# Norm chains begun per residual tile, two norms from one set of tiles, 24 vector products moved into the heads, output in four pieces

## The reference

```python
def rmsnorm(x, g):
    xf = x.astype(jnp.float32)
    y = xf * lax.rsqrt(jnp.mean(xf * xf, axis=-1, keepdims=True) + EPS)
    return (y * g.astype(jnp.float32)).astype(x.dtype)
...
    mod = sc @ w_ada[l] + b_ada[l]
    sh1, sc1, ga1, sh2, sc2, ga2 = jnp.split(mod, N_ADA, axis=-1)
    h = _rmsnorm(x, g_mix[l]) * (1.0 + sc1[:, None, :]) + sh1[:, None, :]
    mix = _hybrid_mixer(...)                     # 8 heads: attention and an LRU; norms of both; w_out
    x = x + ga1[:, None, :] * mix
    h = _rmsnorm(x, g_ffn[l]) * (1.0 + sc2[:, None, :]) + sh2[:, None, :]
    x = x + ga2[:, None, :] * _peer(h, ...)      # top-k over product keys, 16384 experts
return _rmsnorm(x, g_final)
```

## Time and profile before

| | |
|---|---|
| median of 3 runs | 3832.76 us (3823.6 to 3842.07) |
| the profiled execution | 3838.9 us; span of its records 3837.2 |
| mean granted clock of TensorE | 0.962 |
| busy: PE, DVE, ACT, POOL | 3595.6, 2425.1, 1333.5, 390.2 us |
| HBM read, written | 791.66 MB, 24.18 MB |

### The profile page before, as it was taken

The page is one execution under the profiler, slowest core; times in us unless marked ns, Lnnn a source line. Parts: engine busy times, 40 slices in busy tenths (PEclk is TensorE's granted clock), DMA queues, the critical chain, the costliest instruction groups (busy, mean ns, idle before and its releaser), DMA issues. The chain is left out here.

```text
span 3837.2 us, 57514 instructions
## 1 busy us (share of the span) xinstructions
PE 3595.6 (94%) x21190; PEld 3148.6 (82%) x21190; DVE 2425.1 (63%) x4274; ACT 1333.5 (35%) x1967; POOL 390.2 (10%) x402
## 2 busy tenths in 40 slices
PE   5799987999989999999999997999999899999997
PEld 1488876778977999999999995666689899999997
DVE  5443454887547777777777776888816541655664
ACT  1233301212234444444444443211113442555553
POOL 3000000420000000000000000677700000000000
PEclk9899999999999999999999998999999996999999
DMA  8566666655665787887888774222247550555543
GB/s 322 196 226 210 221 241 250 227 203 168 234 258 210 285 297 290 301 300 285 298 288 297 289 290 154 77 87 87 88 154 252 213 179 22 180 182 188 186 170 116
DMA packets 123555, 817.73 MB, mean 213 GB/s; under 512 B 13345, under 2 KB 18721, under 8 KB 27169
## 3 DMA queue, kind: packets, MB, share of 16 engines
q1 hardware_dynamic: 105120, 760.26, 55.0%
q10 hardware_dynamic: 18304, 55.64, 3.8%
HBM read 791.66 MB, written 24.18 MB: 213 GB/s over the span
## 5 line engine op out<-in xcount | busy, mean ns | idle before, releaser
L473 PE MATMUL bank<-H,ring 128*128 128x256 f32 x4352 | 981.5, 384 | 44.8 <-ACT H L969 14.4
L473 PEld LDWEIGHTS bank<-H,ring 128*128 128x128 f32 x4352 | 826.5, 192 | 186.9 <-issue 68.5
L1683 DVE TENSOR_TENSOR vlo<-ring,vhi 128x1024 fp32r<-128x1024 f32 x448 | 548.2, 1225 | 312.1 <-ACT vhi L1141 295.5
L1141 ACT ACTIVATE vhi<-ring 128x1024 fp32r<-128x1024 f32 x448 | 475.0, 1061 | 632.8 <-PE bank L543 350.3
L1402 DVE TENSOR_TENSOR wlo<-ring,whi 128x1024 fp32r<-128x1024 f32 x240 | 293.8, 1225 | 324.0 <-ACT whi L946 317.4
L509 PE MATMUL bank<-Hhi,whi 128*128 128x256 f32 x1920 | 482.0, 288 | 16.4 <-DVE Hlo L1413 9.3
L510 PE MATMUL bank<-Hlo,whi 128*128 128x256 f32 x1920 | 475.3, 285 | 0.0
L536 PE MATMUL bank<-vhi,Ghi 128*128 128x512 f32 x1024 | 400.3, 391 | 0.0
L537 PE MATMUL bank<-vhi,Glo 128*128 128x512 f32 x1024 | 399.9, 391 | 0.0
L509 PEld LDWEIGHTS bank<-Hhi,whi 128*128 128x128 f32 x1920 | 370.0, 193 | 22.0 <-issue 16.2
L488 PE MATMUL bank<-Fhi,vhi 128*128 128x256 f32 x1536 | 374.4, 283 | 0.0
(11 more groups left out here) (384 smaller groups left out, 4401.1 us busy)
## 6 DMA issues: line engine op xcount, KB each, us to landing
ring<-in_peer_u SPq DMA_DIRECT2D x128, 1024.0 KB, 5.0
ring<-in_peer_v SPq DMA_DIRECT2D x128, 1024.0 KB, 4.9
arena<-in_w_mod SPq DMA_DIRECT2D x96, 1024.0 KB, 6.7
ring<-in_w_ada SPq DMA_DIRECT2D x80, 1024.0 KB, 4.9
ring<-in_w_qz SPq DMA_DIRECT2D x64, 1024.0 KB, 4.8
ring<-in_w_in SPq DMA_DIRECT2D x40, 1024.0 KB, 4.8
ring<-in_w_mod SPq DMA_DIRECT2D x32, 1024.0 KB, 5.4
ring<-in_ssm_in SPq DMA_DIRECT2D x32, 1024.0 KB, 4.9
```

The costliest lines, as they stand in the source:

```text
L473: last = mm(out, ring[:, pos % R, k, :], rhs[:, k, :], start=(k == 0), stop=(k == KT - 1))
L1141: A(vhi[:, half], v_half(pos, half), ACT.Copy).then_inc(s("vhi_ready"), 1)
L1683: v.tensor_tensor(vlo[:, half], v_half(pos, half), vhi[:, half].bitcast(F32), ALU.subtract)\
```

## The change

- The squares of a norm are made in pieces, `PIECES`: tiles 0 to 3, 4 to 7, 8 to 11, 12 to 14, 15. For ffn, final, l1 and final2 ACT makes a piece as soon as its residual tiles are there (`new_squares`, which waits for the bank that a residual gives free), in the midst of the stage before; PE's sums stand ahead of the meeting instead of behind it. For the merged norm ACT squares two tiles at the end of each head, and PE sums them, with the groups in two banks, after the last head and ahead of the meeting.
- Variance, root and reciprocal are made for one group of 256 columns only (two for the merged norm).
- final and l0 are made from the same tiles: the sums of x squared (WA) and of (g_final x) squared (WB) together; from them DVE makes both reciprocals, and scales x directly with the product of both. The meeting before this norm goes, on POOL too. x itself is scaled by g_final in the next stage, behind DVE's first two fractions.
- The 24 vectors of w_out go into the heads, three per head, into buffers of their own (`head_vec`), loaded by SP behind positions 2, 4 and 6; DVE makes them behind the vector of position 2. SP waits for `head_free`, which DVE grants once just before its first head. w_out keeps its 16 matmul chunks.
- The output goes in four DMAs of 0.5 MB, each when its four tiles are scaled.

```diff
-STAGES = dict(shift_scale=(4, 8, 4, 2), heads=(8, HEADS, 5, 3), w_out=(20, 2, 8, 12), topk=(20, 2, 12, 0),
+STAGES = dict(shift_scale=(4, 8, 4, 2), heads=(8, HEADS, 5, 3), w_out=(8, 2, 8, 0), topk=(20, 2, 12, 0),
...
+PIECES = ((0, 4), (4, 8), (8, 12), (12, 15), (15, 16))
+SQUARES = dict(mix=0, merged=5, ffn=21, final=26, l1=31, final2=36)
+BANK_USES = dict(heads=(8, 8), w_out=(4, 4), topk=(8, 4), tail=(2, 2), hots=(4, 4), early=(8, 8), peer=(48, 48), turn=(4, 4),
+                 ssm=(8, 8), glu=(4, 4), ssm_out=(4, 4), kv=(6, 6), nsa=(16, 16), w_o=(4, 4))
+
+def tile_done(stage, m):
+
+    before = list(BANK_USES)[:list(BANK_USES).index(stage)]
+    return 1 + sum(BANK_USES[b][m % 4 // 2] for b in before) + m // 4 + 1
...
@@ -407,12 +421,14 @@
                 for pos in range(2, 8):
                     load("heads", i, pos, a["w_in"][5 * i + HEAD_W.index(pos)] if pos in HEAD_W else
                          a["w_ada"][32 + 3 * i + HEAD_M.index(pos)])
+                    if pos in (2, 4, 6):
+                        n = pos // 2 - 1
+                        sp.wait_ge(head_free[n], i + 1)
+                        sp.dma_start(head_vec[:, n], a["w_ada"][56 + 3 * i + n].rearrange("p k n -> p (k n)"))\
+                            .then_inc(head_loaded[n], 16)
             with sp.Fori(0, 2) as i:
-                for m in range(4):
-                    for k, pos in enumerate((0, 1, 2, 3, 4)):
-                        src = a["w_out"][8 * i + 2 * m + k // 2] if k in (0, 2) else \
-                            a["w_ada"][56 + 12 * i + 3 * m + (0, 0, 0, 1, 2)[k]]
-                        load("w_out", i, 5 * m + pos, src)
+                for pos in range(8):
+                    load("w_out", i, pos, a["w_out"][8 * i + pos])
...
             plain("w_o", a["w_o"])
-            sp.wait_ge(s("out_ready"), 1)
-            sp.dma_start(a["out"], SQ).then_inc(s("stored"), 16)
-            sp.wait_ge(s("stored"), 16)
+            for j in range(4):
+                sp.wait_ge(s("out_ready"), 4 * j + 4)
+                sp.dma_start(a["out"][:, 4 * j:4 * j + 4, :], SQ[:, 4 * j:4 * j + 4, :]).then_inc(s("stored"), 16)
+            sp.wait_ge(s("stored"), 64)
...
+            def norm_sums(name):
+
+                for p, (lo, hi) in enumerate(PIECES):
+                    pe.wait_ge(s("squares_ready"), SQUARES[name] + p + 1)
+                    for t in range(lo, hi):
+                        last = mm(WA[:, 0:T], ones[:, 0:P], SQ[:, t, :], start=(t == 0), stop=(t == KT - 1))
+                last.then_inc(s("sums_ready"), 1)
+
+            def merged_sums():
+
+                for h in range(HEADS):
+                    for g in range(2):
+                        pe.wait_ge(s("squares_ready"), SQUARES["merged"] + 2 * h + g + 1)
+                        last = mm((WA, WB)[g][:, 0:T], ones[:, 0:P], SQ[:, HEADS * g + h, :], start=(h == 0), stop=(h == HEADS - 1))
+                last.then_inc(s("sums_ready"), 1)
+
+            def final_sums():
+
+                for p, (lo, hi) in enumerate(PIECES):
+                    pe.wait_ge(s("squares_ready"), SQUARES["final"] + p + 1)
+                    for t in range(lo, hi):
+                        last = mm(WA[:, 0:T], ones[:, 0:P], SQ[:, t, :], start=(t == 0), stop=(t == KT - 1))
+                    if hi == KT:
+                        last.then_inc(s("sums_ready"), 1)
+                    for t in range(lo, hi):
+                        pe.wait_ge(s("scaled_squares"), t + 1)
+                        last = mm(WB[:, 0:T], ones[:, 0:P], SQ2[:, t, :], start=(t == 0), stop=(t == KT - 1))
                 last.then_inc(s("sums_ready"), 1)
...
+            pe.wait_ge(s("attn_ready"), HEADS + 1)
+            merged_sums()
             meet(pe, met)
-            norm_sums("merged", 2)
             pe.wait_ge(s("merged_scaled"), 1)
             with pe.Fori(0, 2) as i:
...
+            def squares(p, src):
+
+                lo, hi = PIECES[p]
+                A(SQ[:, lo:hi, :], src[:, lo:hi, :], ACT.Square).then_inc(s("squares_ready"), 1)
+
+            def new_squares(stage, p):
+
+                for m in range(*PIECES[p]):
+                    act.wait_ge(bank_free[m % 4], tile_done(stage, m))
+                squares(p, x)

             def norm_sqrt(name):
                 n = NORMS[name]
                 act.wait_ge(s("var_ready"), n + 1)
-                A(sd[:], var[:], ACT.Sqrt).then_inc(s("sd_ready"), 1)
+                groups = slice(0, 2) if name == "merged" else slice(1, 2) if name == "l0" else slice(0, 1)
+                A(sd[:, groups], var[:, groups], ACT.Sqrt).then_inc(s("sd_ready"), 1)
...
                 A(M[:, bass.ds(i, 1), :], WA[:, 0:T], ACT.Copy).then_inc(s("attn_ready"), 1)
+                act.drain()
+                A(SQ[:, bass.ds(i, 1), :], M[:, bass.ds(i, 1), :], ACT.Square).then_inc(s("squares_ready"), 1)
+                act.wait_ge(s("lru_done"), i + 2)
+                A(SQ[:, bass.ds(HEADS + i, 1), :], M[:, bass.ds(HEADS + i, 1), :], ACT.Square)\
+                    .then_inc(s("squares_ready"), 1)
             meet(act, met)
-            act.sem_inc(s("norm_src"), 1)
-            norm_squares("merged", M)
             norm_sqrt("merged")
+            for p in range(5):
+                new_squares("w_out", p)
             meet(act, met)
-            act.sem_inc(s("norm_src"), 1)
             act.dma_start(k12, a["k12"]).then_inc(s("k_loaded"), 16)
-            norm_squares("ffn", x)
             norm_sqrt("ffn")
             norm_bias(1, mod[:, 48:64])
...
-            meet(act, met)
-            act.dma_start(disc, a["disc"]).then_inc(s("disc_loaded"), 16)
-            act.dma_start(CC, a["ssm_c"]).then_inc(s("disc_loaded"), 16)
-            act.sem_inc(s("norm_src"), 1)
-            norm_squares("final", x)
+            for p, (lo, hi) in enumerate(PIECES):
+                new_squares("turn", p)
+                if p == 0:
+                    act.dma_start(disc, a["disc"]).then_inc(s("disc_loaded"), 16)
+                    act.dma_start(CC, a["ssm_c"]).then_inc(s("disc_loaded"), 16)
+                for k in range(lo, hi):
+                    A(SQ2[:, k, :], x[:, k, :], ACT.Square, scale=V("g_final")[:, k:k + 1]).then_inc(s("scaled_squares"), 1)
             norm_sqrt("final")
-            norm_squares("l0", x)
             norm_sqrt("l0")
...
             for g in range(1, 16):
                 high("ssm_out", 0, 3 * (g // 2) + g % 2, g)
+                if g in (5, 9, 13):
+                    new_squares("ssm_out", g // 4 - 1)
+            new_squares("ssm_out", 3)
+            new_squares("ssm_out", 4)
             meet(act, met)
...
@@ -1418,18 +1466,16 @@
                 n = NORMS[name]
                 groups = 2 if name == "merged" else 1
                 dve.wait_ge(s("sums_ready"), n + 1)
-                v.tensor_scalar(var[:, 0:groups], WA[:, 0:groups * T].rearrange("p (a b) -> p a b", b=T),
-                                1.0 / width, EPS, ALU.mult, ALU.add)
-                if groups == 1:
-                    v.tensor_scalar(var[:, 1], WA[:, 0:T], 1.0 / width, EPS, ALU.mult, ALU.add)
+                for g in range(groups):
+                    v.tensor_scalar(var[:, g], (WA, WB)[g][:, 0:T], 1.0 / width, EPS, ALU.mult, ALU.add)
                 dve.drain().then_inc(s("var_ready"), 1)
                 dve.wait_ge(s("sd_ready"), n + 1)
-                v.reciprocal(rstd[:], sd[:])
+                v.reciprocal(rstd[:, 0:groups], sd[:, 0:groups])
                 dve.drain()
...
+            for n in range(3):
+                dve.sem_inc(head_free[n], 1)
...
                 whole_vec("heads", i, 2, 32 + 3 * i)
+                for n in range(3):
+                    dve.wait_ge(head_loaded[n], 16 * (i + 1))
+                    for half in range(2):
+                        w = head_vec[:, n, D // 2 * half:D // 2 * half + D // 2]
+                        ins = v.tensor_tensor_reduce(w, w, cond[:, D // 2 * half:D // 2 * half + D // 2], 1.0, 0.0,
+                                                     ALU.mult, ALU.add, accum_out=head_sums[:, half, n:n + 1])
+                    ins.then_inc(head_free[n], 1)
+                dve.drain()
+                v.tensor_copy(mod_ab[:, :, bass.ds(56 + 3 * i, 3)], head_sums[:])
                 dve.wait_ge(s("scores_ready"), i + 1)
...
                 for g in range(8):
-                    m = g // 2
-                    if g > 0:
-                        residual("w_out", i, g - 1, 5 * ((g - 1) // 2) + 2 * ((g - 1) % 2), mod[:, 32:48])
-                    if g % 2 == 0:
-                        whole_vec("w_out", i, 5 * m + 1, 56 + 12 * i + 3 * m)
-                    else:
-                        whole_vec("w_out", i, 5 * m + 3, 57 + 12 * i + 3 * m)
-                        whole_vec("w_out", i, 5 * m + 4, 58 + 12 * i + 3 * m)
-                residual("w_out", i, 7, 17, mod[:, 32:48])
+                    residual("w_out", i, g, g, mod[:, 32:48])
             meet(dve, met)
...
```

(28 more changed lines are left out.)

59 lines of the change are left out of this document (25 added, 34 removed).

## The result

| | before | after |
|---|---|---|
| median | 3830.97 us (4 runs, 3823.6 to 3842.07) | 3784.43 us (4 runs, 3783.76 to 3785.44) |
| ratio | | 0.9876, 95% interval 0.9852 to 0.9901 |
| the profiled execution | 3838.9 us, span 3837.2 | 3783.76 us, span 3782.0 |
| mean granted clock of TensorE | 0.962 | 0.966 |

The changed kernel is 46.5 us faster by the medians, 47.5 us by the ratio; the forecast was 3789. The spans of the two profiled executions differ by 55.2 us; the profiled execution of the kernel before lay 7.9 us above its median. The table cuts both spans at the same events of the timeline; its last column is the prediction's term. In the experiments, "merged" alone is the time from PE's first sum of squares of the merged norm to w_out's first product, 21.07 us in the changed kernel.

What follows compares the result with a forecast made beforehand. TensorE, computing in 94% of the span, was taken as the bound, idling mostly in the norms' chains. Seven gains summed to 44.2 us, off a median of 3832.8 giving 3788.6, stated as 3789; range 3778 to 3808.

Steps and rivals of the forecast that it cites:

- Heads, 0: Eight heads: three extra vectors each fit DVE's idle time, third landing 8.9 us after issue, one us before scores; 0 us.
- the 2.3 us of slack behind the scores: Heads: some 2.3 us more before PE asks for the probabilities, so lateness begins to cost at a landing of about 460.
- The heads-pay rival (13 us): Heads: transfers come late, as in w_out, and cost 13 us, giving 3802; chance 0.15.
- Merged, 6.0: Norm after the heads: sums done 6.9 us earlier, less 0.9 for the modulation addition now showing; gain 6.0 us.
- w_out, 5.3: Stage after the heads: 24 of 40 transfers go, so 5.6 us without work go, less 0.3; gain 5.3 us.
- Ffn, 1.2: Norm after w_out: early sums, but POOL's four products hold DVE's small operations; gain 1.2 us, ends 0 and 7.4.
- Joint norm, 19.3: Final and l0 become one: 64 sums directly behind PE's transposes, then a short chain to the next product; gain 19.3 us.
- l1, 4.5: Norm l1: squares hide in the stage before; four DMA issues (2.2 us) and a table load precede the root; gain 4.5 us.
- final2, 4.7: Last norm: early sums, then meeting, table load, root and reciprocal, scaling at 3819.3 instead of 3824.01; gain 4.7 us.
- output, 3.2: Final store: the last 0.52 MB piece lands 3.0 us after its issue, where the store took 6.2; gain 3.2 us.
- Unchanged stretches, 0: Start, top-k to experts, state space to ssm_out, kv to w_o: no term in the sum, 0 us.
- The signs that were to show it: New profile: heads 39.4 us, w_out 116, merged 20, ffn 25, joint 13.5 from last sum, small operations 1 to 2.4.

Runs made afterwards that it cites:

- Experiment 4: Changed kernel with the third extra vector of each head issued behind position 7 instead of position 6: 3790.02 us.
- experiment 1: Changed kernel with the 24 vectors back between w_out's products and the output as one store: 3781.06 us.
- experiment 3: Changed kernel with ffn's small operations ahead of the meeting, table loads ahead at merged, l1 and final2, l1's DMA issues behind the root: 3776.47 us.
- experiment 2: Changed kernel with POOL's first vector product of top-k waiting until DVE has scaled the ffn norm's last tile: 3776.74 us.
- experiment 6: Changed kernel with the early start undone at ffn and final2, and l1 over 512 columns again: ffn 19.33, final2 11.79, l1 16.48 us.
- experiment 5: Changed kernel with final and l0 made one after the other again, both begun per tile and over 256 columns: 3774.84 us.
- experiment 11: Experiment 8's kernel with the joint norm's first product taking a tile at a time, x scaled by g_final in the glu stage: 3751.97 us.
- experiment 7: Changed kernel with experiment 2's wait, and first products after mix, merged and ffn waiting for one tile at a time: 3758.31 us.
- experiment 8: Changed kernel with what paid together: tile-at-a-time first products, early table loads, POOL held, reordered small operations, fifth store: 3748.55 us, ratio 0.9775.
- experiment 10: Changed kernel, unchanged, profiled once more: 3780.25 us.
- experiment 12: Experiment 11's kernel with DVE's fractions behind the second and fourth scan of a tile instead of first and third: 3734.92 us, ratio 0.9736.

## Why the prediction was right

The mechanism held part by part, but that the total came so near, 46.5 us measured by the medians and 44.2 forecast, is partly luck. Between the two profiles, on which the sum was made, the difference is 55.2: what was changed gave 3.8 more than forecast and stretches at which nothing was forecast gave 7.2. The profiled execution before lay 7.9 us above its median, and that took most of the surplus away again. The sizes, one by one:

- **Heads, 0.** Right, and in five of the eight heads by the working given: the third vector landed 8.8 to 9.1 us after its issue, where the forecast had 8.9. In three it took 11.1 to 12.1, and DVE was 1.0 to 2.1 us late where it should have been 1 early; the 2.3 us of slack behind the scores took it up, in the sixth head with 0.3 us to spare. Experiment 4 shows the edge close behind. The heads-pay rival (13 us) is out by experiment 1.
- **Merged, 6.0, measured 4.8.** The sums came as priced. The step that failed is the table load: I charged it at l1 and final2, but here left it under the sums, where it had been. It moved behind the variance and took back 1.28 us, as experiment 3 shows. That is also why the last product of the heads to w_out's first took 21.7 us and not the 20 that were named.
- **w_out, 5.3, measured 7.6.** Under-sized: I took PE's idle time as all that its waits cost. Without the transfers, the busy time fell too, 115.8 to 113.5. Experiment 1 brings back 8.5.
- **Ffn, 1.2, measured 1.9.** The step that the prediction argued longest: the early start brings POOL's four products over DVE. Experiments 2, 3 and 6 each show it. They go further: without the early start the norm would be 5.1 us shorter. All of this norm's gain, and more, is the width, the scaling that POOL no longer meets and the clock; the early start is a loss there as long as POOL is not held (19.33 us without it, 24.45 with it), and worth 1.05 us once POOL is (18.28).
- **Joint norm, 19.3, measured 20.0.** Right. The heading under which I put it was not: joining is 5.3 of it; the early start, the half width and the meeting that is gone are 14.7 (experiment 5).
- **l1, 4.5, measured 5.4; final2, 4.7, measured 4.6; output, 3.2, measured 3.8.** The four DMA issues at l1 took 1.9 us instead of 2.2, and the last store landed 2.6 us after its issue where I had 3.0. Of l1's gain 1.8 is the width. At final2 the early start gave only 0.7 against the execution of experiment 6, where the clock did not fall and the table load was hidden.
- **Unchanged stretches, 0, measured 7.2 between the two profiles.** The expert products alone gained 6.2, and that repeats; see below. The stages ahead of them gave some 2 back in this pair of profiles. The rest is scatter of the loads at the start and of the later stages.

The signs that were to show it (heads of 39.4 us, small operations of 1 to 2.4, 13.5 us from the last joint sum) came as named, except w_out, 113.5 and not 116, and the merged norm.

## What to carry to other kernels

A chain that is begun earlier also lets its neighbour's work begin earlier: here POOL's products moved from beside the sums onto the chain itself, and one wait on POOL was worth more (6.2 us) than the early start (1.05). Where all of a product's inputs are made one by one, let the product wait for one at a time: 6 us a norm at merged and ffn, more than most of the restructuring. At the joint norm it gave nothing (experiment 11), because the work behind the product started no earlier. And look at every profile by stretches before trusting a difference of totals: an unchanged stage with two paces hid 13 us in experiments 1 and 5.

## What the runs showed of the hardware that I had not expected

- **A stage with two paces.** The same code of the state-space stretch took 584.3 and 585.3 us in two executions (experiments 1 and 5), 594.6 to 594.9 in five, and 597.2 to 597.5 in five. At the slow pace PE waits for a scan of DVE in every tile (15 waits, 15.0 us in all), at the quick one in hardly any (2 waits, 3.5 us); the profiles of experiments 2, 3, 7, 8 and 10 changed from one to the other within the stage. The two differ by 13 us over 16 tiles, 0.8 us a tile. What differs inside is one operation: the first of each pair with which DVE makes its fractions. Behind the third scan of a tile it takes 1.11 us on average at the slow pace and 0.55 at the quick one, and other DVE operations of the stage keep their length. The groups by shape, over 190 us of the stage, of the changed kernel and of experiment 1 (the last numbers before the idle time are busy us and mean ns):

```profile
L1865 DVE TENSOR_SCALAR var<-iota_t,arena 128x256 f32<-128x256 f32 x16 | 17.8, 1114 | 2.2 <-issue 2.2
...
L1861 DVE TENSOR_SCALAR var<-iota_t,arena 128x256 f32<-128x256 f32 x16 | 8.8, 547 | 1.8 <-issue 1.8
```

  In experiment 12 it is 0.74, and the one for the other half of the tile 0.43 instead of 0.66. In the changed kernel it can be seen beside a product of POOL that began 0.1 us ahead of it:

```profile
2574.68 1.26 POOL L2158 TENSOR_TENSOR arena<-arena,y 128x512 f32<-128x512 f32 x1 [0.65 <-DVEq L1898]
2574.78 1.31 DVE L1865 TENSOR_SCALAR var<-iota_t,arena 128x256 f32<-128x256 f32 x1 [0.23 <-issue]
```

  So the slow pace is one in which these operations are held by POOL for longer. What makes an execution fall into it, or leave it halfway, is not shown.

  The kernel before spreads over 25 us (3820.8 to 3845.5) in its runs, and this is likely a part of it, though neither of its two profiles caught the quick pace.
- **Unchanged products got quicker.** The expert products take 1028.0 us from first to last in both profiles of the kernel before, and 1021.8 in the changed one. A group of 24 split products takes 2.87 us before and mostly 2.83 after. The timeline of PE, two group ends before and two after:

```profile
1563.34 1.12 PE L493 MATMUL bank<-Fhi,vlo 128*128 128x256 f32 x8
1566.21 1.00 PE L493 MATMUL bank<-Fhi,vlo 128*128 128x256 f32 x7
```

```profile
1545.07 1.11 PE L510 MATMUL bank<-Fhi,vlo 128*128 128x256 f32 x8
1547.90 1.11 PE L510 MATMUL bank<-Fhi,vlo 128*128 128x256 f32 x8
```

  The lines are the same; the change lays out a new tensor of six columns ahead of many others, so their addresses move. Whether that is the cause was not tried. It is a gain of 6 us that nothing in the diff is about.
- **The clock after a short gap is not a matter of the gap alone.** Gaps of 1.80 and 2.02 us left it at 1.00 (experiment 6, final2 and ffn), one of 1.90 us in the kernel before (final2) was followed by 0.50 for 3 us, and so in both of its profiles. The same sums cost 7.1 or 8.8 us by it.
